# Delta scan of a hybrid decoder layer: keys times state first, then the inverse on a difference of values

## The reference

```
m = tril(k_beta @ k.T * decay, -1)
t_inv = inverse(I + m)
u = t_inv @ (v * beta)
w = t_inv @ (k_beta * exp(g))
v_new = u - w @ state
o = (q * exp(g)) @ state + a_intra @ v_new
state = state * exp(g_last) + (k * exp(g_last - g)).T @ v_new
```

## Times and profile before

| | |
|---|---|
| median of 3 runs | 1860.92 us (1860.22 to 1861.11) |
| profiled execution | 1859.46 us |
| its span | 1857.6 us |
| TensorE clock granted | 0.998 of full speed |
| TensorE products, busy | 1830.2 us, 99% |
| TensorE weight loads, busy | 1467.8 us, 79% |
| VectorE busy | 1247.8 us, 67% |
| ScalarE busy | 750.9 us, 40% |

### The profile page before, as it was taken

The page is one execution under the profiler, slowest core; times in us unless marked ns, Lnnn a source line. Parts: engine busy times, 40 slices in busy tenths (PEclk is TensorE's granted clock), DMA queues, the critical chain, the costliest instruction groups (busy, mean ns, idle before and its releaser), DMA issues.

```text
span 1857.6 us, 23921 instructions
## 1 busy us (share of the span) xinstructions
PE 1830.2 (99%) x8878; PEld 1467.8 (79%) x8878; DVE 1247.8 (67%) x2072; ACT 750.9 (40%) x1261; POOL 265.4 (14%) x385
## 2 busy tenths in 40 slices
PE   8999999999999999999999999999999999999997
PEld 6877767788888888888778777677887888888886
DVE  6856789854475667575878658898534657575748
ACT  3163343322334635454531533533123346354454
POOL 2221111111120010000012211111112201100000
PEclk9999999999999999999999999999999999999999
DMA  6432113322441794766522322223225308856654
GB/s 239 146 126 85 62 63 98 88 80 69 145 150 46 210 255 138 202 181 170 166 100 93 125 74 69 69 89 97 80 69 190 138 13 249 226 150 191 194 135 102
DMA packets 87041, 240.22 MB, mean 129 GB/s; under 512 B 19920, under 2 KB 32400, under 8 KB 85904
## 3 DMA queue, kind: packets, MB, share of 16 engines
q1 hardware_dynamic: 46656, 171.76, 26.7%
q0 software_dynamic: 10368, 37.75, 10.9%
q10 hardware_dynamic: 29904, 29.19, 4.8%
HBM read 227.62 MB, written 11.06 MB: 128 GB/s over the span
## 4 chain that ended last, share of the span: by engine, by line
PE 90%; DVE 4%; ACT 3%; issue 2%; DMA 1%; DVEq 0%; POOL 0%; ACTq 0%; SPq 0%
PE psD L1229 24%; PE psD L1231 23%; PE psD L1230 23%; PE psM L1229 3%; PE psM L1230 3%; PE psM L1231 3%; PE psM L1288 1%; PE psM L1294 1%; PE psM L1507 1%; PE psM L1386 1%; PE psM L1525 1%; PE psM L1513 1%; PE psM L1378 1%; ACT wide L1757 1%; DVE wide L2536 1%
## 5 line engine op out<-in xcount | busy, mean ns | idle before, releaser
L1229 PE MATMUL psD<-a_hi,w_hi 128*128 128x512 f32 (+2 forms) x1488 | 595.3, 400 | 0.9 <-DVE w_lo L1094 0.6
L1231 PE MATMUL psD<-a_hi,w_lo 128*128 128x512 f32 (+2 forms) x1488 | 575.1, 386 | 0.0
L1230 PE MATMUL psD<-a_lo,w_hi 128*128 128x512 f32 (+2 forms) x1488 | 574.2, 386 | 0.0
L1094 DVE TENSOR_TENSOR w_lo<-raw,w_hi 128x1024 fp32r<-128x1024 f32 x216 | 263.5, 1221 | 142.6 <-POOL w_hi L1196 98.0
L1229 PEld LDWEIGHTS psD<-a_hi,w_hi 128*128 128x128 f32 (+1 forms) x1488 | 278.9, 187 | 79.3 <-issue 21.6
L1231 PEld LDWEIGHTS psD<-a_hi,w_lo 128*128 128x128 f32 (+1 forms) x1488 | 278.8, 187 | 57.8
L1230 PEld LDWEIGHTS psD<-a_lo,w_hi 128*128 128x128 f32 (+1 forms) x1488 | 279.2, 188 | 56.7 <-issue 4.8
L2524 DVE TENSOR_TENSOR d_lo<-d_raw,d_hi 128x1024 fp32r<-128x1024 f32 x102 | 124.1, 1222 | 69.2 <-ACT d_hi L2054 69.2
L1196 POOL TENSOR_SCALAR w_hi<-raw 128x1023 fp32r<-128x1023 f32 x150 | 166.2, 1108 | 0.0
L1195 POOL TENSOR_TENSOR w_hi<-raw,tabs 128x1 fp32r<-128x1 f32 x150 | 34.9, 233 | 896.3 <-PE psD L1231 865.3
L1203 POOL DMA_DIRECT2D d_raw<-in_wd x72 | 63.3, 961 | 642.8 <-DMA d_raw<-in_wd 437.7
(11 more groups left out here) (301 smaller groups left out, 2786.5 us busy)
## 6 DMA issues: line engine op xcount, KB each, us to landing
raw<-in_ws SPq DMA_DIRECT2D x216, 512.0 KB, 3.5
d_raw<-in_wd SPq DMA_DIRECT2D x88, 512.0 KB, 5.9
d_raw<-in_wd POOLq DMA_DIRECT2D x72, 512.0 KB, 8.4
s_raw<-in_wo ACTq DMA_DIRECT2D x14, 512.0 KB, 11.5
tabs<-in_tab SPq DMA_DIRECT2D x2, 2880.0 KB, 12.0
x<-rows_d ACTq DMA_DIRECT2D x4, 1024.0 KB, 5.7
x<-out ACTq DMA_DIRECT2D x2, 2048.0 KB, 8.4
x<-in_x SPq DMA_DIRECT2D x4, 512.0 KB, 5.4
```

Of the source, the lines that this page charges most:

```text
L1094: dve.tensor_tensor(w_lo[:, s, :], raw[:, s, :], w_hi[:, s, :].bitcast(F32), ALU.subtract) \
L1229: pe.matmul(out, lhi, rhi, start=start, stop=False, skip_group_check=more)
L1230: pe.matmul(out, lhi, rlo, start=False, stop=False, skip_group_check=more)
L1231: return pe.matmul(out, llo, rhi, start=False, stop=stop, skip_group_check=more)
```

## The change

w is not formed any more. For n = 1, 2, 3 the step ks multiplies the keys with the state (by_heads, L1285), ku on VectorE scales that by beta * exp(g) into bw slot 8 and takes it from the values in place, in two passes that depend on each other, and v2 then is one product of the inverse with the difference. The steps Kp and wT go, on all three engines. ks needs the keys with the feature on the partitions, so kn and K of chunks 1 and 2 come after ks; those of chunk 3 are not made at all. The semaphores Kp and wTn are replaced by Ku, which counts both passes of ku. In schedule() the steps, their costs and dependencies are changed to match, so all orders of the mixing part are computed anew. The levels of the inverse stay as they are. Left out below are three lines that enter the steps in tables.

```diff
@@ -223,13 +223,16 @@
         op("dve", "decay", n, t=4 * read(1, slow), after=[("act", "decay", n)])
     for n in range(ST):
         for i, (x, t) in enumerate((("vn", .44), ("kk", .9), ("kq", .9), ("kn", .44))):
+            if x == "kn" and n:
+                continue
             drains = {"vn": ("dve", "vb", n), "kk": ("dve", "MT", n), "kq": ("dve", "AT", n), "kn": ("act", "K", n)}
             op("pe", x, n, t=t, to=drains[x], after=[("dve", "AT", n - 1)] + [("dve", "decay", n)] * (i > 0))
         op("act", "E", n, t=copied(), after=[("dve", "decay", n)])
         op("dve", "vb", n, t=read(4, 1.1), after=[("pe", "vn", n)])
         op("dve", "MT", n, t=read(4, slow) + read(), after=[("act", "E", n), ("pe", "kk", n), ("dve", "vb", n)])
         op("dve", "AT", n, t=read() + read(4, slow), after=[("pe", "kq", n), ("dve", "MT", n), ("act", "decay", n)])
-        op("act", "K", n, t=copied(), after=[("pe", "kn", n), ("act", "E", n)])
+        if n == 0:
+            op("act", "K", n, t=copied(), after=[("pe", "kn", n), ("act", "E", n)])
         if n + 2 < ST:
             op("act", "decay", n + 2, t=copied(), after=[("dve", "AT", n)])
             op("dve", "decay", n + 2, t=4 * read(1, slow), after=[("act", "decay", n + 2), ("dve", "decay", n + 1)])
@@ -260,16 +263,16 @@
             else:
                 op("pe", "xt", n, l, t=.55, to=("dve", "XT", n, l), after=[("act", "left", n, l), ("act", "XT", n, l - 1)])
                 op("dve", "XT", n, l, t=read(2, 1.2), after=[("pe", "xt", n, l)])
-        over = [("pe", "wT", n - 1)] if n >= 2 else []
         if n:
-            op("dve", "Kp", n, t=read(4, slow), after=[("act", "K", n), ("dve", "Kpp", n - 1)] + over)
+            op("pe", "ks", n, t=.9, to=("dve", "ku", n), after=[("dve", "St", n - 1), ("dve", "AT", ST - 1)])
+            op("dve", "ku", n, t=read(4, 1.1) + read(4, slow), after=[("pe", "ks", n), ("dve", "vb", n), ("dve", "Kpp", n - 1)])
+            if n < ST - 1:
+                op("pe", "kn", n, t=.44, to=("act", "K", n), after=[("pe", "ks", n)])
+                op("act", "K", n, t=copied(), after=[("pe", "kn", n)])
         if n < ST - 1:
-            op("dve", "Kpp", n, t=read(4, slow), after=[("act", "K", n), ("dve", "Kp", n), ("dve", "AT", ST - 1)])
-        if n:
-            op("pe", "wT", n, t=.9, to=("act", "wT", n), after=[("dve", "XT", n, LEVELS - 1), ("dve", "Kp", n)])
-            op("act", "wT", n, t=copied(), after=[("pe", "wT", n)])
-        op("pe", "v2", n, t=1.8 if n else .9, to=("act", "v2", n),
-           after=[("dve", "XT", n, LEVELS - 1), ("dve", "vb", n), ("act", "wT", n), ("dve", "St", n - 1)])
+            op("dve", "Kpp", n, t=read(4, slow), after=[("act", "K", n), ("dve", "AT", ST - 1)])
+        op("pe", "v2", n, t=.9, to=("act", "v2", n),
+           after=[("dve", "XT", n, LEVELS - 1), ("dve", "vb", n)] + [("dve", "ku", n)] * (n > 0))
         op("act", "v2", n, t=copied(), after=[("pe", "v2", n)])
         op("pe", "oT", n, t=1.8 if n else .9, to=("act", "oT", n), after=[("act", "v2", n), ("dve", "AT", n), ("dve", "St", n - 1)])
         op("act", "oT", n, t=copied(), after=[("pe", "oT", n)])
@@ -878,7 +881,7 @@
 
         MT, AT = [bw[:, n, :] for n in range(ST)], [bw[:, ST + n, :] for n in range(ST)]
         eg = [bw[:, 8 + i, :] for i in range(2)]
-        B = {"misc": bw[:, 8, :], "va": bw[:, 9, :], "rows": bw[0:2 * ST * H, 8, 0:P], "Kp": bw[:, 8, :], "St": bw[:, 9, :]}
+        B = {"misc": bw[:, 8, :], "va": bw[:, 9, :], "rows": bw[0:2 * ST * H, 8, 0:P], "Ku": bw[:, 8, :], "St": bw[:, 9, :]}
         gcr, br_ = [xw[:, n, :] for n in range(ST)], [xw[:, ST + n, :] for n in range(ST)]
         for i in range(2):
             for j, n in enumerate(("X", "XT")):
@@ -1035,8 +1038,8 @@
                 return [(f"X{a[0] % 2}", 2 * inner_count(*a))]
             if k == "xt":
                 return [(f"XT{a[0] % 2}", level_count(*a))]
-            if k == "wT":
-                return [("wTn", a[0])]
+            if k == "ks":
+                return [("Ku", 2 * a[0] - 1)]
             if k == "v2":
                 return [("vnew", a[0] + 1)]
             if k == "oT":
@@ -1459,26 +1462,17 @@
                                 pe.wait_ge(*on(s, v))
                             turn_heads(("xt", n, l), lambda h: B["X", n % 2][:, cut(h)])
 
-                    def scan_w(n):
-                        pe.wait_ge(*on(f"XT{n % 2}", level_count(n, LEVELS - 1)))
-                        pe.wait_ge(*on("Kp", n))
-                        by_heads(("wT", n), lambda h: B["Kp"][:, cut(h)], lambda h: B["XT", n % 2][:, cut(h)])
+                    def scan_k(n):
+                        pe.wait_ge(*on("St", n))
+                        by_heads(("ks", n), lambda h: kB(h, n), lambda h: B["St"][:, cut(h)])
 
                     def scan_v(n):
 
                         pe.wait_ge(*on(f"XT{n % 2}", level_count(n, LEVELS - 1)))
                         pe.wait_ge(*on("vb", n + 1))
                         if n:
-                            pe.wait_ge(*on("wTn", n))
-                            pe.wait_ge(*on("St", n))
-                        ps = small_bank(("v2", n))
-                        for h in range(H):
-                            ins = pe.matmul(ps[:, cut(h)], B["XT", n % 2][:, cut(h)], qkv[:, 2 * H + h, cut(n)],
-                                            start=True, stop=n == 0)
-                            if n:
-                                ins = pe.matmul(ps[:, cut(h)], B["P1", n % 2][:, cut(h)], B["St"][:, cut(h)],
-                                                start=False, stop=True)
-                        small_done(ins)
+                            pe.wait_ge(*on("Ku", 2 * n))
+                        by_heads(("v2", n), lambda h: B["XT", n % 2][:, cut(h)], lambda h: qkv[:, 2 * H + h, cut(n)])
 
                     def scan_o(n):
                         pe.wait_ge(*on("vnew", n + 1))
...
@@ -1854,9 +1848,6 @@
                     def turned(n, l):
                         sig(act.copy(B["XT", n % 2], mid(act, ("xt", n, l))[:, :]), f"XT{n % 2}")
 
-                    def scan_w(n):
-                        sig(act.mul(B["P1", n % 2], mid(act, ("wT", n))[:, :], -1.0), "wTn")
-
                     def scan_v(n):
                         sig(act.copy(MT[n], mid(act, ("v2", n))[:, :]), "vnew")
 
...
@@ -2298,14 +2289,16 @@
                         sig(dve.tensor_tensor(odd, odd, ps[0:HALF, 0:H * HALF].rearrange("p (h c) -> p h c", h=H),
                                               ALU.subtract), f"XT{i}")
 
-                    def kp_(n):
-                        if n == 1:
+                    def ku(n):
+                        v, t = qkv[:, 2 * H:, cut(n)], heads(B["Ku"])
+                        ps = mid(dve, ("ks", n))
+                        if n > 1:
+                            own("Ku")
+                        else:
                             own("bk")
-                        else:
-                            mid(dve, ("wT", n - 1))
-                        dve.wait_ge(*on("K", n + 1))
-                        sig(dve.tensor_tensor(heads(B["Kp"]), qkv[:, 0:H, cut(n)], over(egl[:, n * H:(n + 1) * H], P),
-                                              ALU.mult), "Kp")
+                        sig(dve.tensor_tensor(t, heads(ps[:, :]), over(egl[:, n * H:(n + 1) * H], P), ALU.mult), "Ku")
+                        own("Ku")
+                        sig(dve.tensor_tensor(v, v, t, ALU.subtract), "Ku")
 
                     def kpp(n):
                         k = qkv[:, 0:H, cut(n)]
@@ -2313,9 +2306,7 @@
                             dve.wait_ge(*on("esm", 3))
                             own("qs")
                             sig(dve.tensor_tensor(egl, beta, egc, ALU.mult), "bk")
-                            dve.wait_ge(*on("K", 1))
-                        else:
-                            own("Kp")
+                        dve.wait_ge(*on("K", n + 1))
                         sig(dve.tensor_tensor(k, k, over(kps[:, n * H:(n + 1) * H], P), ALU.mult), "Kpp")
 
                     def sd(n):
...
```

More of the change, by code:

```diff
@@ L1555, in _ @@
                              "unit": unit, "va_turn": va_turn, "cv": cv_, "rs": rs, "rv": rv, "rows": rows,
-                             "vn": vn, "kk": kk, "kq": kq, "kn": kn, "left": left, "xx": xx, "xt": xt, "wT": scan_w,
+                             "vn": vn, "kk": kk, "kq": kq, "kn": kn, "left": left, "xx": xx, "xt": xt, "ks": scan_k,
                              "v2": scan_v, "oT": scan_o, "st": st, "index": index, "as": as_,
@@ L1962, in _ @@
                              "mt_out": mt_out, "blk_in": blk_in, "y_out": y_out, "x_in": x_in_, "left": left, "XT": turned,
-                             "wT": scan_w, "v2": scan_v, "oT": scan_o,
+                             "v2": scan_v, "oT": scan_o,
                              "index": index, "sexp": sexp, "prob": prob, "pt": pt_, "attend": attend, "fin_sq": fin_sq, "fin": fin,
@@ L2447, in _ @@
```

(2 more changed lines are left out.)

## The result

The changed kernel takes 1863.96 us, median of 20 runs (1862.83 to 1866.65), the one before 1860.89 us (1858.08 to 1861.95). The ratio is 1.0021 (95% interval 1.0014 to 1.0027): 3.1 us slower, where 5.7 us faster was forecast. The time lies above the range. The profiled execution took 1865.82 us.

A forecast was written before the change was run, and what follows sets the result against it. TensorE, busy 99% of 1857.6 us, was taken to bound the kernel. Terms -5.4 - 0.86 + 0.6 = -5.7 us gave a median of 1855.2 us, 0.31% faster, with an 8-in-10 range of 1851.5 to 1861.8 us.

The forecast's parts named there:

- Bound: TensorE always has something to run through the scan, so each microsecond of small products removed lets later ones start earlier.
- step 2: v2 on TensorE goes from 16 records to 8, 0.90 us each in six places: 5.4 us less.
- the sum: Total of the priced parts: -5.4 - 0.86 + 0.6 = -5.7 us, for a median of 1855.2 us.
- Steps 1 to 3: TensorE: ks replaces wT at 0; v2 halves, 5.4 us less; chunk 3's kn transposes go, 0.86 us less.
- Step 4: One more break per chunk in TensorE's projection stream, 0.09 us each: 0.6 us more, bounds 0 and 2.4 us.
- Steps 5 and 6: VectorE swaps Kp for two-pass ku, net 2.2 us a layer, off the path; ScalarE loses wT's eviction and a copy: 0.
- Step 7: Scan chain from state to v2 is 5.5 us longer per layer, covered by projection work through an earlier start: 0.
- the two runs of pure projection: Stretches on TensorE just ahead of the scan, 43.9 us together, taken as filler of which 5.5 us are wanted.
- The first rival: Freed time turns into TensorE waits or breaks at the scan's handoffs; no change, 1858 to 1862 us; chance 0.25.
- the signs listed for step 7: Wait over 1 us before ks, v2 or the norms of B, or TensorE under 43 of 44 us in the scan.
- signs of being right: TensorE: 8822 records, 5 to 7 us less busy, waits for ku or the state under 0.5 us each.
- The slower rival: The scan's chain ends last and TensorE stands before the norms of B; +5.3 us, 1866.2 us; chance 0.11.

The follow-up runs named there:

- v2_twice: cover_back with the 8 records of a second, overwritten product put back into v2 of chunks 1 to 3; 1861.18 us, ratio 0.9999 to the kernel before.
- cover_out: Kernel before, old arithmetic, with oT(0), st(0) and chunk 1's last level put ahead of mergeC(0), as in the changed kernel; 1868.85 us, ratio 1.0044.
- ku_thrice: cover_back with the first pass of ku made twice, 0.7 us longer in each of six chunks; 1854.1 us, its repeat 1855.28 us.
- gate_after: Changed kernel with gate slab mgate(A,3) moved behind mergeC(3), ahead of merge(A,0); 1859.87 us, ratio 0.9999 to the kernel before.
- cover_back: Changed kernel with one planner edge: oT of chunk 0 waits for the last slab of mergeC; 1856.41 us, ratio 0.9978 to the kernel before; its repeat 1855.71 us.
- gate_before: Kernel before the change with gate slab mgate(A,3) moved behind mergeC(3); 1865.08 us, ratio 1.0028.
- cover_v2: Changed kernel with v2 of chunk 0 held behind the last slab of mergeC by a planner edge; 1857.17 us, ratio 0.9982 to the kernel before.
- cheap_rank: Changed kernel with only the planner's costs of ks and ku set to 0.01 us, so all is reordered; 1860.96 us, ratio 1.0000 to the kernel before.

## Why the prediction was wrong

- Bound (TensorE, start to start): right. v2_twice confirms the price of step 2, 5.5 us for 5.4. The whole saving, 5.7 us in the sum, is 4.3 us in the one pair with equal holes (cover_out against the changed kernel), an interval that holds 5.7, too.
- Steps 1 to 3 (ks for wT, half of v2, kn of chunk 3): right by the count of records, 56 fewer.
- Step 4 (breaks): the projection products that are followed after 0.30 to 0.35 us are 153 in the profile before and 162 in the one after. 9 more at 0.09 us are 0.8 us, for 0.6 forecast. Steps 2 and 3 less 4.3 us would leave 2.0 us for it, inside its bounds; what the other 1.2 us are, if they are real, is open.
- Steps 5 and 6 (VectorE, ScalarE): right. ku's two passes took 0.69 us each and start 0.7 us apart; with a third pass nothing changes.
- Step 7, the chain: right in that it is covered (ku_thrice). The handoff of 0.25 us in it is the planner's figure; at the one place looked at, from the end of y_lo to the product that waits for it, the rows show 0.10 us. The rank rose and the scan began earlier, as written. What failed is the sentence after it, that beginning earlier costs 0, and with it the last one of the part, "what the new order can cost or give is of the size of the waits that are there, under 1 us a layer either way". It measured +2.7 us of waits and 1.4 to 2.5 us of clock a layer, 9.3 us added up in this one execution; cover_out, with the same hole, lost 8.2 us by its ratio. Against it stand the 4.3 to 5.7 us saved.

I read the two runs of pure projection, 24.7 and 19.2 us, as filler that the scan could draw on, and didn't ask what parted them. Between 405.05 and 410.41 stand small blocks one after another with two short waits, the only ones of the scan; I read one of them and left out the other. A place where a planner that has slabs uses none is a place where, in its order of slabs, none can run. The small products there were not being covered; they were the cover. The waits of 0.2 and 0.6 us were the sign that the cover was used up: 2.6 us of products were drawn out, and the waits grew by 2.7.

The first rival had the right kind (freed time turns into waits) and not the size: it took waits of 1.2 us a layer (the row's 1.2 us is both layers together) and stopped at -1.5 us, since it laid them at handoffs of the scan. It also left out the clock. None of the signs listed for step 7 came: the waits opened before xx(2,5) and merge(A,0), and not before ks, v2 or the norms of B. What came were signs of being right, 8822 records and no wait for ku; only TensorE's busy time, 0.3 us less where 5 to 7 were named, spoke against the forecast. The slower rival, which was put at 0.11, is the wrong mechanism: TensorE never stood before the norms of B for want of slabs, and in the changed kernel, too, it is busy for all 44.00 us of the stretch from 430 to 474 us. That its direction came true was luck.

## What to carry to other kernels

In a kernel whose order a list scheduler writes, look for the places where it ran small work back to back although large pieces were left: there, as here, something may hold all large pieces up, and the small work is the cover. A change that makes a chain longer raises the rank of its head and can pull that cover out, though the chain itself costs nothing; a held-back edge for those steps is then worth more than the arithmetic (here 7.5 us against 4 to 5). When waits on a full TensorE are priced, add what the lower clock costs behind them.

## What the runs showed of the hardware

The fall of the clock wasn't expected. After 1.69 and 1.82 us of waits within 5.1 us it fell in both layers of the changed kernel, for 1.4 and 2.5 us of lost time, and in both layers of cover_out, for 1.5 and 1.6. With the waits filled by idle products it didn't fall.

With shorter waits the same order of work goes either way. gate_after waits 1.5 us ahead of mergeC(0), 1.30 of them in one piece, in both layers; the clock fell in layer 0 (0.83 over 380 to 390 us) and not in layer 1. The order of cover_back, with one wait of 0.77 us in the hole, was profiled in five executions (cover_back, its repeat, v2_twice, ku_thrice and its repeat), two holes in each: it fell in layer 1 of v2_twice and of ku_thrice, for 1.5 and 1.4 us, and in none of the other eight. It didn't fall with 0.22 and 0.61 us (before), with 1.64 and 0.46 (gate_before), with 1.31 (cover_v2) or with 0.96 and 0.33 (cheap_rank), in one profiled execution each. So what decides isn't settled here, and such a fall belongs to the spread of the times, too: the profiled execution of ku_thrice, with the fall, took 1859.6 us, where the median of its runs was 1854.1.
